# A twelfth 2 MB place for the expert weights, two places and the first reused one loaded in halves, and a first expert gather split over two PSUM banks

## The reference

```
h = x + hybrid_mixer(rms_norm(x), ...)             # two kinds of attention, gates, output projection
hn = rms_norm(h)
logits = hn @ w_router + b_router                  # 1024 x 32
top_vals, top_idx = top_k(logits, 4); gates = softmax(top_vals)
per expert e, for the tokens that chose it:
    hgu = xb @ w_gate_up[e] + b_gate_up[e]         # 1024 x 2048
    gate = min(hgu[:, :1024], 7); up = clip(hgu[:, 1024:], -7, 7)
    act = (up + 1) * gate * sigmoid(1.702 * gate)
    y = act @ w_down[e] + b_down[e]                # 1024 x 1024
h = h + sum over chosen experts of gate * y
```

## Time and profile before

| | |
|---|---|
| time, median of 3 runs | 1159.17 us (1157.65 to 1160.5) |
| the profiled execution | 1161.69 us, its span 1159.9 us |
| PE busy | 1093.5 us (94%), mean granted clock 0.993 |
| DVE, ACT, POOL busy | 260.5, 140.7, 9.8 us |
| moved by the DMA engines | 435.66 MB (10^6 bytes), mean 376 GB/s |
| issue to landing of a 2 MB piece | median 46 us |

### The profile page before, as it was taken

The page is one execution under the profiler, slowest core; times in us unless marked ns, Lnnn a source line. Parts: engine busy times, 40 slices in busy tenths (PEclk is TensorE's granted clock), DMA queues, the critical chain, the costliest instruction groups (busy, mean ns, idle before and its releaser), DMA issues.

```text
span 1159.9 us, 11496 instructions
## 1 busy us (share of the span) xinstructions
PE 1093.5 (94%) x5084; PEld 472.4 (41%) x5084; DVE 260.5 (22%) x610; ACT 140.7 (12%) x242; POOL 9.8 (1%) x18
## 2 busy tenths in 40 slices
PE   7999999999999999999999989999999999999997
PEld 3676778543333333333333333333333333333332
DVE  1574322222221111111211111111111111111111
ACT  2315331001000000000000000000000000000000
POOL 1100000000000000000000000000000000000000
PEclk9999999989999999999999999999999999999999
DMA  9456534789999999999999999999999999999994
GB/s 271 150 207 229 193 142 174 294 336 425 429 427 429 427 427 427 428 428 428 427 428 427 429 425 428 427 428 427 427 427 427 428 428 427 429 427 429 428 426 204
DMA packets 44355, 435.66 MB, mean 376 GB/s; under 512 B 6192, under 2 KB 7376, under 8 KB 19632
## 3 DMA queue, kind: packets, MB, share of 16 engines
q1 hardware_dynamic: 43888, 434.29, 89.7%
q0 software_dynamic: 96, 0.08, 0.2%
q10 hardware_dynamic: 320, 0.53, 0.1%
HBM read 433.85 MB, written 1.05 MB: 375 GB/s over the span
## 4 chain that ended last, share of the span: by engine, by line
PE 59%; DMA 36%; DVE 2%; ACT 1%; issue 0%; another core or an unknown queue 0%; SPq 0%; ACTq 0%; DVEq 0%
PE Pp L750 20%; DMA ring<-in_w_gate_up 15%; DMA unit<-in_w_gate_up 12%; PE Bp L764 11%; DMA att_pair<-in_w_gate_up 8%; PE Pp L471 7%; PE Ap L778 4%; PE Bp L736 3%; PE Pp L459 3%; PE Pp L639 2%; PE Ap L650 2%; PE Pp L498 1%; PE Bp L757 1%; DVE G L1220 1%; DMA unit<-in_w_in 1%; PE Pp L698 1%
## 5 line engine op out<-in xcount | busy, mean ns | idle before, releaser
L750 PE MATMUL Pp<-ring,OBT 128*64 128x512 f32 x1120 | 253.7, 600 | 23.9 <-DMA ring<-in_w_gate_up 23.9
L1209 DVE TENSOR_SCALAR G<-Pp 128x512 f32<-128x512 f32 x32 | 22.1, 692 | 668.3 <-PE Pp L750 668.3
L750 PEld LDWEIGHTS Pp<-ring,OBT 128*64 128x64 f32 x1120 | 78.5, 138 | 186.6 <-issue 137.3
L764 PE MATMUL Bp<-ring,G 128*64 128x512 f32 x560 | 125.4, 595 | 2.3 <-DVE G L1220 1.1
L750 PE MATMUL Pp<-unit,OBT 128*64 128x512 f32 x352 | 79.7, 595 | 7.2 <-DMA unit<-in_w_gate_up 7.2
L471 PE MATMUL Pp<-norm_pair,unit 128*128 128x256 f32 x384 | 85.2, 380 | 0.0
L1408 ACT ACTIVATE G<-G 128x512 f32<-128x512 f32 x32 | 20.2, 630 | 503.7 <-DVE G L1209 503.7
L471 PEld LDWEIGHTS Pp<-norm_pair,unit 128*128 128x128 f32 x384 | 72.1, 190 | 10.9 <-issue 1.1
L764 PEld LDWEIGHTS Bp<-ring,G 128*64 128x64 f32 x560 | 38.7, 137 | 76.6 <-issue 70.4
L778 PE MATMUL Ap<-G,cst 64*128 64x512 f32 x264 | 65.6, 615 | 1.4 <-ACT G L1415 1.4
L736 PE MATMUL Bp<-X,cst 128*64 128x512 f32 x240 | 56.6, 593 | 0.0
(11 more groups left out here) (218 smaller groups left out, 840.1 us busy)
## 6 DMA issues: line engine op xcount, KB each, us to landing
ring<-in_w_gate_up SPq DMA_DIRECT2D x70, 2048.0 KB, 46.0
ring<-in_w_down SPq DMA_DIRECT2D x35, 2048.0 KB, 47.3
unit<-in_w_gate_up SPq DMA_DIRECT2D x22, 2048.0 KB, 46.2
more<-in_w_gate_up SPq DMA_DIRECT2D x12, 2048.0 KB, 46.1
unit<-in_w_down SPq DMA_DIRECT2D x12, 2048.0 KB, 44.8
att_pair<-in_w_gate_up SPq DMA_DIRECT2D x12, 2048.0 KB, 47.2
norm_pair<-in_w_gate_up SPq DMA_DIRECT2D x12, 2048.0 KB, 46.4
unit<-in_w_in SPq DMA_DIRECT2D x7, 2048.0 KB, 7.7
```

What stands on the lines that cost most here:

```text
L750: last = mm((Gps, Ups)[q // 2][64 * (q % 2):64 * (q % 2) + 64, :], xT[:, k % 4, k // 4, :], w[:, q * 512:(q + 1) * 512], start=False, stop ...
L764: last = mm(Yps[64 * hf:64 * hf + 64, :], hT[:, c, s, :], w[:, c * 1024 + hf * 512:][:, 0:512], start=s == 0 and c == 0, stop=s == DN - 1 ...
L1209: V.tensor_scalar(gm, Gps, LIMIT, None, ALU.min).then_inc(d_gm, 1)
```

## The change

`PLACES` goes from 11 to 12. With 12 places and 6 turns an expert, turn t takes the place of turn t-12, the same piece of the expert two before.

The **twelfth place** is 16 KB a partition of a new tensor `gate_rest` of 24 KB: its first 16 KB are G, and the place is columns 2048 to 6143, that is the half of G that the experts do not use and 8 KB behind it, named `once`. `once` holds what is needed only until the experts start: the constants of the mixer (`cst_once`, loaded by a transfer of its own), KAT, the router weights, the tables of ranks, the norm gains, the router bias. So `cst` shrinks to 1188 columns, and the constants come in two transfers (`in_c` is now waited for at 32).

**Halves.** `load_half` moves 1 MB, columns 0 to 2047 or 2048 to 4095 of a place. Turns 10 and 11 have their first halves issued right behind turn 7 (place 10's is `BG`, place 11's the second half of G, both no longer read). Their second halves wait for the router products (`m_lr`) and for the ranks (`m_rk`). Turn 12, the first piece of expert 2, goes to place 0 in halves: the first when PE has used the first half of turn 0 (a new semaphore `gu_first`), the second when it has used all of it. `full_count` lets readers wait for the right number.

**The first gather.** The zeroing products are removed: the first `scatter` of each bank now has the start flag, so that it overwrites. The gather for the first expert writes features 0 to 3 of each row pair to the bank `Tps` and the rest to the upper half of `Yps` (`first_tokens`), four products each; DVE takes the first bank after `m_g0` while PE fills the second, and PE's first gate/up products wait for the first take alone (`d_x0`), those from k = 4 on for the second (`d_xt`). The second bank also held the rank sums, so its gather waits for `v_rk`. The router products are 128 columns wide instead of 32 (96 of the columns are not read).

The diff, without the renaming of slices:

```diff
-PLACES = 11
+PLACES = 12
+HALVED = (10, 11)
...
-        cst = sb("cst", [P, C_W])
+        cst = sb("cst", [P, C_KEPT])
...
-        att_pair = sb("att_pair", [P, 2048 + 2304])
-        att, qkv = att_pair[:, 0:2048], att_pair[:, 2048:2048 + 2304]
+        att_pair = sb("att_pair", [P, 4096])
+        att, qkv = att_pair[:, 0:2048], att_pair[:, 2048:4096]
...
-        G = sb("G", [P, KC, 2, SEQ])
+        gate_rest = sb("gate_rest", [P, 6144])
+        gflat = gate_rest[:, 0:4096]
+        G = gflat.rearrange("p (c r t) -> p c r t", c=KC, r=2)
+        once = gate_rest[:, 4096:6144]
+        cst_once = once[:, 0:C_W - C_KEPT]
+        KAT = once[:, 576:832]
+        wide_router = once[:, 832:832 + KC * NE + P - NE]
...
-                  norm_pair[:, :]]
+                  norm_pair[:, :], gate_rest[:, 2048:6144]]
...
+        def first_tokens(r):
+            return (Tps[:, 0:256], Yps[:, 256:512])[r].rearrange("p (c s) -> p c s", c=4)
+
+        def full_count(turn):
+            halves = turn % PLACES in HALVED or (turn % PLACES == 0 and turn >= PLACES)
+            return 16 * (turn // PLACES + 1 + halves)
...
-                    sp.dma_start(cst[:, P:], consts[:, P:]).then_inc(in_c, 16)
+                    sp.dma_start(cst[:, P:], consts[:, P:C_KEPT]).then_inc(in_c, 16)
+                    sp.dma_start(cst_once, consts[:, C_KEPT:]).then_inc(in_c, 16)
...
+            def load_half(turn, h):
+                e, i = divmod(turn, TURNS)
+                src = gu_src(e, i) if i < GU else dn_src(e, i - GU)
+                part = slice(2048 * h, 2048 * h + 2048)
+                sp.dma_start(places[turn % PLACES][:, part], src[:, part]).then_inc(place_full[turn % PLACES], 16)
...
             load(7)
+            sp.wait_ge(bias_ok, 2)
+            load_half(10, 0)
+            load_half(11, 0)
             sp.wait_ge(m_wo, 4)
             load(8)
             load(9)
-            sp.wait_ge(bias_ok, 2)
             sp.wait_ge(m_lr, TB)
-            load(10)
-
-            for turn in range(PLACES, TURNS * BREAK + PLACES):
+            load_half(10, 1)
+            sp.wait_ge(m_rk, TB)
+            load_half(11, 1)
+
+            sp.wait_ge(gu_first, 1)
+            load_half(PLACES, 0)
+            released(PLACES)
+            load_half(PLACES, 1)
+            for turn in range(PLACES + 1, TURNS * BREAK + PLACES):
                 released(turn)
                 load(turn)
...
-                    last = mm(Pp[:, 0, b * NE:(b + 1) * NE], XT[:, k, b * P:(b + 1) * P], WR[:, k, :],
+                    last = mm(Pp[:, 0, b * P:(b + 1) * P], XT[:, k, b * P:(b + 1) * P],
+                              wide_router[:, k * NE:k * NE + P],
                               start=k == 0, stop=k == KC - 1, skip_group_check=True)
...
-            pe.wait_ge(z_ok, 1)
-            for bank in range(4):
-                mm(Ap[:, bank, :], zero[:, 0:P], zero[:, P:], start=True, stop=False, skip_group_check=True)
             pe.wait_ge(bias_ok, 2)
             biases()
             pe.wait_ge(d_oh, 2)
-            gather_block(Tps, 1, 0, KC).then_inc(m_ga, 1)
+            gather_first(1, 0).then_inc(m_g0, 1)
+            pe.wait_ge(v_rk, 1)
+            gather_first(1, 1).then_inc(m_ga, 1)
...
-                pe.wait_ge(d_xt, e + 1)
                 if e:
+                    pe.wait_ge(d_xt, e + 1)
                     pe.wait_ge(a_gt, e)
                     biases()
+                else:
+                    pe.wait_ge(d_x0, 1)
                 for k in range(KC):
+                    if e == 0 and k == 4:
+                        pe.wait_ge(d_xt, 1)
                     if k % 2 == 0:
                         w = piece(TURNS * e + k // 2)
                     last = gate_up(w[:, (k % 2) * 2048:(k % 2 + 1) * 2048], k)
+                    if e == 0 and k == 0:
+                        last.then_inc(gu_first, 1)
...
                     for b in range(TB):
-                        scatter(b)
+                        scatter(b, start=True)
...
+            def take_first():
+                for r, (taken, done) in enumerate(((m_g0, d_x0), (m_ga, d_xt))):
+                    dve.wait_ge(taken, 1)
+                    V.tensor_tensor(xT[:, :, r, :], first_tokens(r),
+                                    gpair[:, 4 * r:4 * r + 4].unsqueeze(2).to_broadcast([P, 4, SLOTS]), ALU.mult)\
+                        .then_inc(done, 1)
```

More of the change, by code:

```diff
@@ L59 @@
 NTM = 1224
-C_ID, C_LNEG, C_ONEG, C_STRICT, C_ONES = 0, 128, 256, 384, 512
-C_SLOT, C_ADM, C_CAUSAL = 640, 768, 1280
-C_COS, C_SINN, C_SIN, C_E32, C_OFF = 1664, 1696, 1712, 1728, 1760
-C_EYE = 1764
-C_W = 1796
+C_ID, C_SLOT, C_ADM, C_CAUSAL, C_OFF, C_EYE = 0, 128, 256, 768, 1152, 1156
+C_KEPT = 1188
+C_LNEG, C_ONEG, C_STRICT, C_ONES = 1188, 1316, 1444, 1572
+C_COS, C_SINN, C_SIN = 1700, 1732, 1748
+C_W = 1764
 def shape_constants():
@@ L166, in hybrid_block @@
         hT = hTf.rearrange("p (c r s) -> p c r s", c=4, r=2)
-        ofl = cst[:, C_ADM:C_COS]
+        ofl = cst[:, C_ADM:C_OFF]
         GT = ofl[:, 0:256]
@@ L189, in hybrid_block @@
         ident = cst[:, C_ID:C_ID + P]
-        lneg = cst[:, C_LNEG:C_LNEG + P]
-        oneg = cst[:, C_ONEG:C_ONEG + P]
-        strict_ones = cst[:, C_STRICT:C_STRICT + 2 * P].rearrange("p (a q) -> p a q", a=2)
+        lneg = cst_once[:, C_LNEG - C_KEPT:][:, 0:P]
+        oneg = cst_once[:, C_ONEG - C_KEPT:][:, 0:P]
+        strict_ones = cst_once[:, C_STRICT - C_KEPT:][:, 0:2 * P].rearrange("p (a q) -> p a q", a=2)
         slots = cst[:, C_SLOT:C_SLOT + P]
@@ L383, in _ @@
                 for turn in range(TURNS * BREAK, TURNS * BREAK + PLACES):
-                    sp.wait_ge(place_full[turn % PLACES], 16 * (turn // PLACES + 1))
+                    sp.wait_ge(place_full[turn % PLACES], full_count(turn))
                 with sp.Fori(0, NE) as e:
@@ L687, in _, with gather_first @@
             turn_h(1, 1)
-            def gather_block(out_bank, b, k0, k1):
-                for k in range(k0, k1):
-                    last = mm(out_bank[:, at_slots(k):at_slots(k) + SLOTS], features(X[:, b, :], k), OH[:, b, :],
+            def gather_first(b, r):
+                for k in range(4 * r, 4 * r + 4):
+                    last = mm(first_tokens(r)[:, k % 4, :], features(X[:, b, :], k), OH[:, b, :],
                               start=b == 0 and k == 0, stop=b == 1, skip_group_check=True)
@@ L701, in _ @@
             pe.wait_ge(d_oh, 1)
-            gather_block(Tps, 0, 0, 4)
+            gather_first(0, 0)
             router_products(1, 1)
@@ L772, in turn_gates, with scatter @@
                 return tr(Gps[:, P:SEQ], PG[:, 1, :], ident)
-            def scatter(b, stop=False):
+            def scatter(b, start=False, stop=False):
                 for hf in range(2):
@@ L778, in scatter @@
                     last = mm(Ap[:, 2 * b + hf, :], GT[h, b * P:(b + 1) * P], ysb[h, :],
-                              start=False, stop=stop, skip_group_check=True)
+                              start=start, stop=stop, skip_group_check=True)
                 return last
             def piece(turn):
-                pe.wait_ge(place_full[turn % PLACES], 16 * (turn // PLACES + 1))
+                pe.wait_ge(place_full[turn % PLACES], full_count(turn))
                 return places[turn % PLACES]
@@ L885, in _ @@
             for b in range(TB):
-                scatter(b, True).then_inc(m_end, 1)
+                scatter(b, stop=True).then_inc(m_end, 1)
         @block.vector
@@ L1042, in b_softplus @@
                     d = SPt[:, r, :].rearrange("p (g q) -> p g q", g=3)[:, 0:3:2, :]
-                    last = V.tensor_tensor(d, d, cst[:, C_STRICT:C_STRICT + P].unsqueeze(1).to_broadcast([P, 2, P]),
+                    last = V.tensor_tensor(d, d, strict_ones[:, 0:1, :].to_broadcast([P, 2, P]),
                                            ALU.mult)
@@ L1259, in _ @@
             dve.wait_ge(g_pr, 1)
-            take_expert(0)
+            take_first()
             for b in range(TB):
```

35 lines of the change are left out of this document (16 added, 19 removed).

## The result

| | before | after |
|---|---|---|
| median, 6 runs each | 1159.68 us (1157.35 to 1163.19) | 1152.88 us (1151.78 to 1154.52) |
| the profiled execution, its span | 1161.69, 1159.9 us | 1153.17, 1151.4 us |
| mean granted clock | 0.993 | 0.997 |
| moved | 435.66 MB, mean 376 GB/s | 435.65 MB, mean 378 GB/s |

The ratio is 0.9944 (95%: 0.9925 to 0.9963): 6.8 us less by the medians, where 1151.7 us, 7.5 us less, was forecast. The whole interval lies on the faster side of 1, though its end nearest to 1, 0.37% less, is only just past the 0.3% that a measurement of this kernel can tell.

The account below looks back on a forecast made before the run. The prediction took the DMA queue, full from 300 us, and its earlier idle time as the bound. Gains of 4.9 + 2.7 = 7.6 us took the median from 1159.17 to 1151.6, written as 1151.7 us; range 1149.8 to 1156.2.

Parts of the forecast that it names:

- The bound: DMA queue full from 300 us at 428 GB/s; the end is set by its earlier idle time plus a fixed rest.
- the sum of 7.6: Total gain forecast at the kernel's end: 4.9 us from 224 to 236 us plus 2.7 us from 250 to 254 us.
- The first gap: Queue nearly idle from 224 to 236 us, worth 10.0 us; two early halves of 1.05 MB win 4.9 us.
- The second gap: Queue short of bytes from 250 to 254 us; closes whole if PE reaches the first expert earlier, 2.7 us.
- The lead: PE starts the first expert's gate/up at 243.5 us instead of 246.06, 2.6 us earlier, with the clock as before.
- The router's wide products: Router products of 128 columns take as long as those of 32: cost 0, at most 2.8 us for 32 records.
- The tightest place: Turn 16, waiting for the first expert's first down piece, has its first byte at 269.1 us, half a microsecond to spare.
- if PE gained nothing: Before the first expert: turn 16 would be 2.1 us late, and 0.6 of the 2.7 us would be left.
- PE gaining nothing: Rival, chance 0.12: wide router products cost 2.8 us ahead of the first expert; gain 5.3 us, time 1153.9 us.
- A clock that stays at half for longer: Same 0.12 rival: some 5 us longer at half clock costs PE 2.5 us; gain 5.5 us, time 1153.7 us.
- Halves as restarts: Rival, chance 0.09: three extra transfers cost some 1.5 us each, 4.5 us; 3.1 us of gain stay, 1156.1 us.
- A full queue that moves less: Rival, chance 0.06: the stream from turn 12 on falls to 419 GB/s, 19 us more, 1170.6 us; decides from 424.4 downward.

Follow-up runs that it names:

- the one that changes the stream itself: The changed kernel with each of the 179 pieces from turn 13 on loaded as two 1 MB transfers: 1165.62 us, ratio 1.0049.
- the two kernels that have PE's new way without early halves: The changed kernel with turns 10 and 11 loaded whole, 1157.70 us; the changed kernel with 11 places and no early halves, 1157.46 us.
- the old way: The changed kernel with 32-column router products, four products in place of the zeroing ones, and gate/up after both takes: 1155.0 us, ratio 0.9955.
- the narrow router: The changed kernel with router products of 32 columns instead of 128, profiled twice: 1152.37 us, ratio 0.9931; again, one run, 1154.8 us.
- the two variants of the kernel before: The kernel before with turn 10's first half issued early, 1160.08 us; the kernel before with router products of 128 columns, 1158.7 us.

## Why the prediction was right, step by step

**The bound** holds. The stream kept 427 GB/s, the stretch behind the last gate/up piece is the same 27 us, and the changes of rest and missing bytes agree to 0.7 us in the change and in all experiments but the one that changes the stream itself. The time behind turn 4's issue fell by 7.0 and 7.4 us against the sum of 7.6; an estimated 0.2 of the difference are the three transfers.

**The first gap, 4.9 us,** is right. From 224 to 236 us 238 GB/s leave 5.3 us missing, of 10.0. Taking the early halves away cost 4.5 us of rest, 4.8 of the medians. The two halves are issued 1.2 to 1.7 us ahead of the 207 us forecast, most of it by the earlier start. That the queue is dry at 229 us as forecast is luck: I let turns 4 to 7 keep it full until 224 us, while in the kernel before it ran until 225.2 (475 GB/s from 224 to 225 us, 66 in the next), and the start 1.5 us earlier took that back. The size of the gap does not hang on it.

**The second gap, 2.7 us,** is right in size: 143 to 432 GB/s, and 2.3 to 2.5 us in the two kernels that have PE's new way without early halves. That PE's lead does it is shown by putting the old way back (2.9 us worse by the rest, about 2 by the medians). The lead itself was mis-sized: 4.4 us, where 2.6 were forecast, since I let the gather take its 3.68 us at half clock and it took 2.10 at full. The text had named this possibility and that it would be worth nothing at the end; the narrow router shows both, for with it the lead is 2.7 us and the end alike. So the path, the waits and the end were right, and the size of the lead was right only for a clock that the change did not keep.

**The router's wide products** cost next to nothing, as taken: 1.95 us for 16 records against 1.87, 0.2 us for all 32 records. The upper bound of 2.8 us is ruled out.

**The tightest place.** Turn 16 did not wait in the change: no dent at 269 us, 429 GB/s from 252 to 300. It went out 61.6 us after turn 4 (263.37 - 201.81) where the forecast had 64.9 (268.2 - 203.35), so the margin was an estimated 3.8 us and not half a microsecond. Without the lead the dent is there, but it has company at 250 and 254 us. The forecast's "if PE gained nothing" had 2.1 us of loss at turn 16 and 0.6 of gain left, so 5.5 in all; measured, that kernel came to 4.0 by the rest and 4.8 by the medians. This step looked at one turn, where three stretches lose, and was too mild by 1.5 us of rest.

**The rivals.** PE gaining nothing did not happen: it gained 4.4 us. Its mechanism is real, though, as the old way shows, and by the rest dearer than I priced it. A clock that stays at half for longer, the other half of this rival, did not come either, although products were taken away: the granted clock was 1.00 from 236 to 250 us. Halves as restarts, 1.5 us each: 0.073 us each. The Trainium skill (DMA: Bandwidth & Descriptors, "Anatomy of one DMA") has about 2.0 us of fixed time a transfer, measured there on the GpSimd path. In SP's full queue these runs show 0.073 us, a twenty-seventh of it, and the measurement decides. A full queue that moves less: 427 GB/s with 12 places and with 11 in PE's new way, against 428; nothing near the 424.4 from which that would decide.

**The time.** 1152.88 us lies 1.2 us above the forecast and within its range. The working went from a profiled execution that was 2.5 us above its median. Turn 4 was issued at 203.35 us in it; in the two variants of the kernel before, which have the same work ahead of that point, at 201.18 and 201.03 us. So most of that excess lay in the start, and it was right to carry the 7.6 us over to the median and not the profiled span. By the medians 6.8 came, where 7.5 had been forecast: the median of before, 1159.17 when the forecast was made, is 1159.68 with three more runs.

## What to carry to other kernels

When a transfer queue is full to the end, add up its idle time before it fills, in microseconds of bytes, and count an edit by what it takes off that sum; compute ahead of the fill is worth its time only until it no longer keeps a place from coming free. A load moved ahead needs a second thing, namely that the next place comes free by the time the queue reaches it, or the gap only moves (one half issued early in the kernel before: 0.1 us, within the noise; two of them in the change: 4.5 us). Where kernels differ by under 1%, compare spans from a common event behind the noisy start.

## What the runs showed of the hardware

- **The clock.** PE was busy without a break in both kernels from 224 to 236 us, and yet the granted clock fell to 0.50 by 240 us in the one and stayed at 1.00 in the other. The kernels differ there in the router products, in the four zeroing products, and in the gather with the wait behind it. With the wide products alone it still fell, and so it did with all the rest of the new way but them (mean 0.76 from 236 to 250 us in both, 0.63 with none of it). Which of them holds it, and what the chip looks at, is left open.
- **Small transfers in a full queue.** 1 MB pieces go at 421 GB/s, 2 MB pieces at 427: 144 packets more and 0.073 us for each extra transfer.
- **The start.** The first 32 records of 512 columns take 14.0 to 14.4 us in eleven profiles and 16.0 to 16.5 us in three, at a granted clock of 1.00 in both kinds. This spread of over 2 us is a third of what the change is worth; its cause is not shown.
